# A recurrent scan on one core: 64x64 matmuls laid on other quadrants of TensorE, group norm's sums and spread cut into 64x64 pieces

## The reference, cut to what matters

```python
def frame_step(state, inp):                       # state: heads x 64 x 64
    r_t, w_t, k_t, v_t, a_t, b_t = inp
    sa = jnp.einsum('bhvk,bhk->bhv', state, a_t)
    state = (state * w_t[:, :, None, :] + sa[..., None] * b_t[:, :, None, :]
             + v_t[..., None] * k_t[:, :, None, :])
    y_t = jnp.einsum('bhvk,bhk->bhv', state, r_t)
    return state, y_t
...
mean = jnp.mean(y, axis=-1, keepdims=True)        # over the 64 channels of a head
var = jnp.mean(jnp.square(y - mean), axis=-1, keepdims=True)
y = (y - mean) * lax.rsqrt(var + GN_EPS)
y = y * ln_w.reshape(N_HEADS, HEAD_SIZE) + ln_b.reshape(N_HEADS, HEAD_SIZE)
bonus = jnp.sum(rh * kh * r_k, axis=-1, keepdims=True) * vh
out = ((y + bonus).reshape(bsz, seq, d).astype(h.dtype) * g) @ w_o
```

## Time and profile before

| | us |
|---|---|
| median of 3 runs | 2475.09 (2474.28 to 2475.65) |
| the profiled execution | 2468.86 |
| its span in the trace | 2467.1 |
| TensorE matmul busy / weight load busy | 2411.2 (98%) / 2053.6 (83%) |
| VectorE / ScalarE / GpSimd busy | 1625.7 / 1081.5 / 223.1 |

### The profile page before, as it was taken

The page is one execution under the profiler, slowest core; times in us unless marked ns, Lnnn a source line. Parts: engine busy times, 40 slices in busy tenths (PEclk is TensorE's granted clock), DMA queues, the critical chain, the costliest instruction groups (busy, mean ns, idle before and its releaser), DMA issues.

```text
span 2467.1 us, 43151 instructions
## 1 busy us (share of the span) xinstructions
PE 2411.2 (98%) x18172; PEld 2053.6 (83%) x18172; DVE 1625.7 (66%) x2640; ACT 1081.5 (44%) x1696; POOL 223.1 (9%) x226
## 2 busy tenths in 40 slices
PE   8999999999999999999999999999999999999998
PEld 7787989886678887898989889898678987889888
DVE  7867979667856556675768667575355744557558
ACT  4224454327653334545456333343255544334334
POOL 0100000110220000000000010111221000011010
PEclk9999999999999999999999999999999999999999
DMA  8664565662310003364644345355112431336335
GB/s 318 194 195 136 162 208 183 193 216 69 98 40 4 5 30 128 92 165 120 161 112 135 106 117 165 94 140 159 61 52 69 142 98 48 99 111 159 123 95 142
DMA packets 101057, 304.62 MB, mean 123 GB/s; under 512 B 11280, under 2 KB 13584, under 8 KB 100352
## 3 DMA queue, kind: packets, MB, share of 16 engines
q1 hardware_dynamic: 80944, 237.38, 29.5%
q0 software_dynamic: 19920, 64.48, 10.8%
HBM read 297.62 MB, written 4.19 MB: 122 GB/s over the span
## 4 chain that ended last, share of the span: by engine, by line
PE 84%; DVE 9%; ACT 3%; issue 2%; SPq 1%; DMA 1%; DVEq 0%; ACTq 0%
PE ps L784 19%; PE ps L790 16%; PE ps L788 16%; PE ps L837 5%; PE ps L840 5%; PE ps L842 5%; PE ps L800 3%; PE ps L803 3%; DVE WLs L2127 2%; PE ps L849 1%; ACT WHs L1417 1%; PE ps L999 1%; SPq L3165 1%; PE ps L1012 1%; DMA raw<-in_cw_in_k 1%
## 5 line engine op out<-in xcount | busy, mean ns | idle before, releaser
L2127 DVE TENSOR_TENSOR WLs<-raw,WHs 128x1024 fp32r<-128x1024 f32 (+3 forms) x497 | 507.8, 1022 | 258.7 <-ACT WHs L1417 254.8
L784 PE MATMUL ps<-HH,WHs 128*128 128x512 f32 x1728 | 654.4, 399 | 6.2 <-ACT HH L1512 2.6
L1417 ACT ACTIVATE WHs<-raw 128x1024 fp32r<-128x1024 f32 (+3 forms) x516 | 455.6, 884 | 310.4 <-PE ps L842 140.9
L790 PE MATMUL ps<-HH,WLs 128*128 128x512 f32 x1462 | 570.4, 390 | 2.7 <-DVE WLs L2127 2.7
L788 PE MATMUL ps<-HL,WHs 128*128 128x512 f32 x1462 | 569.4, 389 | 0.0
L784 PEld LDWEIGHTS ps<-HH,WHs 128*128 128x128 f32 x1728 | 323.5, 188 | 79.1 <-issue 12.4
L837 PE MATMUL ps<-HT,WHs 128*128 128x256 f32 x1344 | 375.5, 279 | 5.9 <-DVE X L2214 5.8
L842 PE MATMUL ps<-HT,WLs 128*128 128x256 f32 x1344 | 373.3, 278 | 0.3 <-DVE WLs L2127 0.2
L840 PE MATMUL ps<-HT,WHs 128*128 128x256 f32 x1344 | 373.0, 278 | 0.0
L790 PEld LDWEIGHTS ps<-HH,WLs 128*128 128x128 f32 x1462 | 274.4, 188 | 62.2 <-DVE WLs L2127 4.6
L788 PEld LDWEIGHTS ps<-HL,WHs 128*128 128x128 f32 x1462 | 274.8, 188 | 56.0 <-issue 2.2
(11 more groups left out here) (475 smaller groups left out, 3625.0 us busy)
## 6 DMA issues: line engine op xcount, KB each, us to landing
ada<-in_adaw POOLq DMA_DIRECT2D x80, 512.0 KB, 4.6
raw<-in_f1gu_b SPq DMA_DIRECT2D x20, 512.0 KB, 3.5
raw<-in_f2gu_b SPq DMA_DIRECT2D x20, 512.0 KB, 3.5
raw<-in_f1gu_a_m SPq DMA_DIRECT2D x18, 512.0 KB, 3.5
raw<-in_w_in_m SPq DMA_DIRECT2D x18, 512.0 KB, 3.5
raw<-in_f2gu_a_m SPq DMA_DIRECT2D x18, 512.0 KB, 3.5
ada<-in_adaw SPq DMA_DIRECT2D x16, 512.0 KB, 16.4
raw<-in_cw_in_m SPq DMA_DIRECT2D x16, 512.0 KB, 3.6
```

The lines of the kernel that those rows point to most:

```text
L784: pe.matmul(o[m], WHs[:, s, w], hi, start=k == 0, stop=False)
L790: t = pe.matmul(o[m], WLs[:, s, w], hi, start=False, stop=k == DEPTH_K[name] - 1)
L1417: act.activation(WHs[:, SLOT[v], 0:n], piece(v), ACT.Copy).then_inc(*S.up("w_hi", ("hi", v)))
L2127: dve.tensor_tensor(WLs[:, s, 0:n], piece(v), WHs[:, s, 0:n].bitcast(F32), SUB).then_inc(*S.up("w_lo", ("lo", v)))
```

## The change

The heads of blocks 4 to 7 keep T, XT and w on the other half of the partitions (`j = u ^ hf`), so that streams which take both halves of the heads in turn can use four quadrants. For it `pa` of half 1 is cut into two 64-column matmuls, whose near part goes to the other half; `w`, `ls` and `u` take both halves in one loop, into two banks, with one wait for the later half and one signal for both; the transposes of w's level follow both. The sums of squares and the spread are cut into 64x64 pieces, with the sums now in two banks.

```diff
@@ group
-                if part in ("pa", "pk"):
+                if part == "pa" and hf:
+                    o = bank_two(part, c, hf)
+                    for i, f in enumerate(fs):
+                        ready(c, f)
+                        for x, r in ((L, 0), (R, 1)):
+                            for u in range(2):
+                                for p in range(2):
+                                    j, n = u if r else 1 - u, 128 * i + 64 * r
+                                    t = pe.matmul(o[home(p, j), j, n:n + 64], A[half(p), f, tokens(u)], x[half(p), f, tokens(u)], start=True, stop=True)
+                    t.then_inc(*S.up("mm_scan", ("full", part, c, hf)))
+                elif part in ("pa", "pk"):
...
-                                n = 256 * hf + 64 * i
-                                t = pe.matmul(o[home(p, u), u, n:n + 64], L[half(p), f, tokens(u)], A[half(p), f, tokens(u)],
+                                j, n = u ^ hf, 256 * hf + 64 * i
+                                t = pe.matmul(o[home(p, j), j, n:n + 64], L[half(p), f, tokens(u)], A[half(p), f, tokens(u)],
...
                 elif part == "w":
-                    o = bank("w", c, hf)
-                    on.wait_ge(*S.at("Mak", c, hf))
-                    for i, f in enumerate(fs):
-                        for u in range(2):
-                            on.wait_ge(*S.at("VT", f // 2 * 2, u))
-                            for p in range(2):
-                                n, h, v = 256 * u + 64 * i, home(p, u), 128 * f + 64 * u
-                                t = pe.matmul(o[h, n:n + 64], Mak[h, n:n + 64], VT[h, c, v:v + 64], start=True, stop=True)
-                    t.then_inc(*S.up("mm_scan", ("full", "w", c, hf)))
-                    turned(c, hf, -1)
+                    if hf:
+                        o = [bank("w", c, e) for e in range(2)]
+                        on.wait_ge(*S.at("Mak", c, 1))
+                        on.wait_ge(*S.at("VT", 6, 1))
+                        for i in range(4):
+                            for u in range(2):
+                                for e in range(2):
+                                    for p in range(2):
+                                        n, h, v = 256 * u + 64 * i, home(p, u), 128 * (4 * e + i) + 64 * u
+                                        t = pe.matmul(o[e][home(p, u ^ e), n:n + 64], Makb[(2 * c + e) % 4][h, n:n + 64], VT[h, c, v:v + 64],
+                                                      start=True, stop=True)
+                        t.then_inc(*S.up("mm_scan", ("full", "w", c, 0), ("full", "w", c, 1)))
+                        turned(c, 0, -1)
+                        turned(c, 1, -1)
@@ through
                 if part == "ls" and cc:
-                    for hf in range(2):
-                        o = bank("ls", cc, hf)
-                        on.wait_ge(*S.at("S", cc - 1, hf))
-                        for f, i, p in heads(hf):
-                            t = pe.matmul(o[home(p, u), 64 * i:64 * i + 64], L[half(p), f, cs], ST[half(p), 64 * f:64 * f + 64],
-                                          start=True, stop=True)
-                        t.then_inc(*S.up("mm_scan", ("full", "ls", cc, hf)))
+                    o = [bank("ls", cc, hf) for hf in range(2)]
+                    on.wait_ge(*S.at("S", cc - 1, 1))
+                    for i in range(4):
+                        for hf in range(2):
+                            for p in range(2):
+                                f = 4 * hf + i
+                                t = pe.matmul(o[hf][home(p, u ^ hf), 64 * i:64 * i + 64], L[half(p), f, cs], ST[half(p), 64 * f:64 * f + 64],
+                                              start=True, stop=True)
+                    t.then_inc(*S.up("mm_scan", ("full", "ls", cc, 0), ("full", "ls", cc, 1)))
...
                 if part == "u":
-                    for hf in range(2):
-                        o = bank("u", cc, hf)
-                        on.wait_ge(*S.at("T", c, hf, 4))
-                        on.wait_ge(*(S.at("wk", cc, hf) if cc else S.at("w", c, hf)))
-                        for f, i, p in heads(hf):
-                            h, n = home(p, u), 128 * f + 64 * u
-                            t = pe.matmul(o[h, 64 * i:64 * i + 64], T[h, n:n + 64], Wk[h, 512 * u + 64 * f:512 * u + 64 * f + 64],
-                                          start=True, stop=True)
-                        t.then_inc(*S.up("mm_scan", ("full", "u", cc, hf)))
+                    o = [bank("u", cc, hf) for hf in range(2)]
+                    on.wait_ge(*S.at("T", c, 1, 4))
+                    on.wait_ge(*(S.at("wk", cc, 1) if cc else S.at("w", c, 1)))
+                    for i in range(4):
+                        for hf in range(2):
+                            for p in range(2):
+                                f, j = 4 * hf + i, u ^ hf
+                                h, n = home(p, j), 128 * f + 64 * j
+                                t = pe.matmul(o[hf][home(p, u), 64 * i:64 * i + 64], T[h, n:n + 64], Wk[h, 512 * u + 64 * f:512 * u + 64 * f + 64],
+                                              start=True, stop=True)
+                    t.then_inc(*S.up("mm_scan", ("full", "u", cc, 0), ("full", "u", cc, 1)))
@@ group_norm
-                    o = bank("gsum", c)
+                    o = bank_two("gsum", c)
                     on.wait_ge(*S.at("gsq", c))
                     for f in range(8):
-                        t = pe.matmul(o[:, 2 * f:2 * f + 2], gsq[:, f], bones[:, 0:128:64], start=True, stop=True)
+                        for u in range(2):
+                            for p in range(2):
+                                t = pe.matmul(o[half(u), p, f:f + 1], gsq[half(p), f, 64 * u:64 * u + 64], bones[half(p), 64 * p:64 * p + 1],
+                                              start=True, stop=True)
...
                     for f in range(8):
-                        for p in range(2):
-                            n = 16 * c + 2 * f + p
-                            t = pe.matmul(o[half(p), f // 4, 128 * (f % 4):128 * (f % 4) + 128], ur[:, n:n + 1].to_broadcast([128, 64]),
-                                          ident[:, :], start=True, stop=True)
+                        for u in range(2):
+                            for p in range(2):
+                                n = 16 * c + 8 * p + f
+                                t = pe.matmul(o[half(p), u, 64 * f:64 * f + 64], ur[half(u), n:n + 1].to_broadcast([64, 64]),
+                                              ident[half(u), half(u)], start=True, stop=True)
```

More of the change, by code:

```diff
@@ L1818, in group_norm @@
                     on.wait_ge(*S.at("full", "gsum", c))
-                    act.activation(ur[:, 16 * c:16 * c + 16], taken("gsum", c)[:, 0:16], ACT.Sqrt, scale=1.0 / 64,
+                    act.activation(ur[:, 16 * c:16 * c + 16].rearrange("q (p f) -> q p f", p=2), taken_two("gsum", c)[:, :, 0:8], ACT.Sqrt, scale=1.0 / 64,
                                    bias=eps6[:, 1:2]).then_inc(*S.up("a_scan", ("gr", c), ("free", "gsum", c)))
@@ L2718, in group_norm @@
                     on.wait_ge(*S.at("V3", 7))
-                    gn = taken_two("gn", c).rearrange("p a (f t) -> p (a f) t", t=128)
+                    gn = taken_two("gn", c).rearrange("p u (f t) -> p u f t", t=64)
+                    y = x.rearrange("p f (u t) -> p u f t", u=2)
                     n = 4 if c == 3 else 8
@@ L2724, in group_norm @@
                         free = [("free", "gn", c)] if f + n == 8 else []
-                        dve.tensor_tensor(x[:, fs], x[:, fs], gn[:, fs], MUL).then_inc(*S.up("v_scan", ("gx", c, f), *free))
+                        dve.tensor_tensor(y[:, :, fs], y[:, :, fs], gn[:, :, fs], MUL).then_inc(*S.up("v_scan", ("gx", c, f), *free))
                         on.wait_ge(*S.at("gx", c, f))
```

## The result

The changed kernel takes 2483.8 us (median of 10 runs) against 2475.46 for the kernel before in the same series: a ratio of 1.0039, 95% interval 1.0026 to 1.0053, about 9.7 us slower by the ratio (the two medians lie 8.3 apart). The forecast was 2473.3, no change.

A forecast was written before the change was run, and what follows sets the result against it. The prediction took TensorE's array, then code at 3.6 us per 128 loads, as bounds. By stretch, -0.7 + 0.9 + 0.9 - 2.9 = -1.8 us on 2475.09 gave 2473.3, with its own range 2470 to 2477.

The forecast's parts named there:

- The bounds: In the scan: TensorE's array first, then arriving code, 128 load and matmul pairs per packet of 3.6 us.
- Rival (a): In the scan: code is no bound, the array is; about -15 us, 2460; chance 0.10.
- Rival (d): In the changed streams: the four quadrants take turns in pairs; about +4 us, 2479; chance 0.04.
- The added waits: w waits for the second half's Mak, +0.8 us in chunk 1; ls for the state, leaving gain 0 to 0.2.
- The stalls: In the scan: more and longer TensorE stalls without a releaser, 128 loads apart, together some 10 us more.
- 748 to 826: First stretch of the scan: gains of w and u against Mak's wait and pa's code, -0.7 us; ends -4.2, +2.7.
- 826 to 862: Scan stretch with no time over its code: ls, u, w give 0, pa costs +0.9 us; ends -4, +2.
- 862 to 916: Scan stretch with 160 loads added: 14 + 1.25 packets at 3.6 us, +0.9; ends -6, +4.2.
- 916 to 947: Last stretch of the scan: code is no bound except once; sum -2.9 us, ends -4.3 and 0.
- Sums of chunk 2 and u before it: Before the stall ending at 922.07: a gain of 1.4 us becomes a longer stall, 0, at best -1.4.
- the last spread: Spread of chunk 3, after a wait of 1.08 us for VectorE's reciprocal: its own gain is -1.0 us.
- Rival (c): From 826 to 916: added code is paid at the long turn, 3.82 us a packet; +5.2, 2480.3; chance 0.09.

The follow-up runs named there:

- e3: The kernel before with one four-quadrant stream (level 0 of p, chunk 2) run eight times instead of once, 448 pairs more: 1.0061 of the kernel before.
- f1: e3 with two wide matmuls that compute nothing ahead of each 128 repeated loads, 8 in all: 1.0042 of the kernel before.
- g1: The whole change with 18 wide matmuls that compute nothing, in the longest stalls and before two waits for VectorE: 1.0009 of the kernel before.
- f2: The whole change with 23 wide matmuls that compute nothing, put broadly where it had stalled: 1.0039 of the kernel before.

## Why the prediction was wrong

- *The bounds.* Right. Streams on four quadrants halved (u and ls 0.46 for 0.47, w with its transposes 2.16 for 2.09, sums 0.95 to 1.1 for 0.93, and spread 1.1 where the clock was full). Code is the second bound, but its price was set a little low: 3.73 us a packet in e3 and f1, 3.45 to 3.95 in after where TensorE stalls at both ends of one, and 37.8/10.25 = 3.69 and 56.2/15.25 = 3.69 by stretch, for the 3.6 taken. At 3.73 the prediction's own sum would have been +1.6 instead of -1.8. Rival (a) is out: the ends of packets stand in the open, in e3 by 0.85 and 1.77 us for 128 loads. Rival (d) is out by the streams.
- *The added waits.* Right in kind, and small. Mak of the second half is written by 779.25 and w of chunk 1 starts at 779.37, but TensorE had stalled 0.92 us for code just before, so that the wait for it shows as 0.2 us in the matmul row and not 0.8; w of chunk 2 waits another 0.5. ls of sub-chunk 2 ends 842.51 where it ended 838.03 before, 4.48 later in a trace shifted by 4.81: a gain of 0.3 for 0 to 0.2.
- *The stalls.* Right in size, +9.1 or, with the wait at 924.03, +10.4, for +10; packets up to where 916 was: 45 for 46.
- *By stretch.* 748 to 826: -0.5 for -0.7. 826 to 862: +1.8 for +0.9, its end +2.0. 862 to 916: +2.2 for +0.9, inside its ends. Both come to 3.69 us a packet, the half-clocked work from 874.5 to 881 included.
- *916 to 947* is the step that failed: +2.3 for -2.9, where the ends were -4.3 and 0. "Sums of chunk 2 and u before it ... so a gain of 1.4 turns into a longer stall: 0": the one stall of 1.12 became two, 1.42 (which ends just ahead of this stretch) and 2.62, and behind the first the clock fell to half, from 925.3 to 935.5 (0.50 from 926 to 934). State and y of sub-chunk 6, 29 ns a load elsewhere, took 52 to 55. From u to the gate's first matmul after is slower by 4.4 us (937.39 - 924.98 = 12.41 against 924.72 - 916.68 = 8.04), and behind it faster by 2.1. There the forecast gains came in part: the last spread, counted as a gain of 1.0, started after a wait of 1.70 for VectorE's reciprocal instead of 1.08 and took 951.54 - 949.60 = 1.94 at half clock (0.50 from 950 to 952), as long as its old form at the full one. Of the -2.9, 0.6 for u of sub-chunk 7 and 0.3 for ls are terms that no run shows; what the traces show, from the start of one stream to the start of the next, is u at 940.75 - 940.27 = 0.48 (granted clock 1.00) for 929.29 - 927.94 = 1.35 (0.50 from 928 to 930), and the ls ahead of it at 935.76 - 934.85 = 0.91 (0.61 from 934 to 936) for 923.18 - 922.42 = 0.76 (1.00).
- *The missing term.* The sum treated the clock as given. A stall was priced at its own length alone. Across the timed executions of all these kernels the time falls by 1.65 us per 0.001 of mean clock (one slope fitted to 193 executions, one level for each kernel; standard error 0.12). Between before and after lie 0.991 - 0.987 = 0.004, 6 to 7 of the 9.7 us by this slope; at equal clock after is some 3 to 4 us over before. The fit shows that time and clock go together, not which drives the other; that the clock has a part of its own rests on f1 and g1. By estimate from the mean clocks and the level of 0.50, 0.004 of mean clock is 0.008 of the time at half clock, and at most half of that is lost: 2470 x 0.004 = 10. The slope gives two thirds of it, which fits e3, where the half clock cost little while code was the bound (28 ns a load at half clock, 29 the pace of code).
- *Rival (c)*, slower by the long turn of code, had the right sign and, at 2480.3, half of the loss. The turn measured, 3.69 to 3.73, lies between the forecast's 3.6 and its 3.82, but without the clock it falls short.

What stays open is why the clock falls behind one stall and not behind the next, and how the changed kernel's 3 to 4 us at equal clock divide among its stalls.

## What to carry to other kernels

Count instructions before quadrants: here a stream of small matmuls that already ran at 128 load and matmul pairs per 3.6 to 3.7 us gained nothing from a faster array, and cutting one matmul into four cost code even where it halved the array's time (sums 0.95 us for 1.87, with 48 pairs more). Price a stall not by its length alone but with the half-clocked work behind it (6.5 us at 0.51 behind the stall of 1.35 in after), and read the granted clock by short stretches, because a half-clocked stream at the pace of code looks busy and free of stalls (9.60 of 10 us busy at 0.53 in e3). Where a stall can't be removed, a wide matmul put into it can be worth more than it costs (g1: 9.5 us of them, 6.8 us faster), but only if it fits (f2: 12 us of them, nothing won).

## What was not expected of the hardware

- Beside a transfer of weights the next packet of code came later: 6.2 us between two packets beside a burst of 1.5 MB (in before and in after), 5.3 beside 1 MB, 3.3 to 4.1 elsewhere in after where TensorE waits half a microsecond or more for it.
- The clock fell behind stalls of 0.6 to 1.5 us each: in after four of them (0.59, 1.48, 0.83, 1.35) lie between 859 and 874.5 us, and then the granted clock is 0.51, with the engine's row full (by stretch):

```profile
874.50:881.00 6.50, 6.48 (x181) 6.34 (x181) 2.27 (x5) 0.49 (x1) 0.00 (x0) 0.51 0.02 5
```

- The same kernel spent 20.5 us of one scan at half clock and 34.1 of another, and its times spread over 16 us (2479.9 to 2496.2), those of before over 10.
